# Moving the latent norms and index queries of a sparse attention ahead of the early merge products

## The chip, the cores and the metric

The kernel runs on one core of a Trainium2 chip. The metric is the device time of one execution in microseconds. The engines are PE (TensorE), DVE (VectorE), ACT (ScalarE), POOL (GpSimd) and SP (SyncE), whose queue issues most of the DMAs. They run side by side, each through its own list of instructions in order, and wait for each other on semaphores only.

## The reference

One decoder layer over 512 tokens of width 1024: adaLN conditioning, a mixer of three branches, and a mixture of experts with a shared expert. All data is float32. The mixer projects the normalised input h once and computes

- branch A, a gated linear attention (four heads), branch C, an mLSTM (four heads), each normalised per head and gated;
- branch B, a sparse attention over a latent. What matters of it here:

```
cq  = rms(h @ w_cq)  * norm_q      # 256 channels: "cn 0, 1"
ckv = rms(h @ w_ckv) * norm_kv     # 128 channels: "cn 2"
q_idx = (cq @ w_qi) / sqrt(32)     # 8 index heads of 32
I[t, s] = sum_h w[t, h] * relu(q_idx[t, h] . k_idx[s])      # causal
sel  = top 128 keys of I[t]
attention of 8 heads over ckv[sel], with q = cq @ w_uq taken through w_uk, and ALiBi
```

- the merge `(g_a * ya + g_b * yb + g_c * yc) @ w_o`, where each y is a branch times its up matrix and each g is a sigmoid of 1024 channels of h's projection.

Then come residual, norm, router (top 6 of 64 experts in groups), the experts and the final norm.

## The kernel before

**Layout.** Activations are held transposed, channels on the 128 partitions and 512 tokens along the free dimension, so that a projection of 128 channels is one PSUM bank of 128 x 512. Projections of h use float32 values split in two parts (hi and lo): `triple` (L892) makes hi x hi and hi x lo of eight k-tiles (16 matmuls, L899), then lo x hi (8 matmuls, L904). The hi part of each weight block is made by ACT (`split_hi`, L1393), the lo part by DVE (L1767) or, for the early gates, by POOL (`split_lo`, L718, in four pieces). Other products are plain float32, which PE makes in two passes per matmul.

**What orders the work.** `product_order()` (L57) is one list of all products, in PE's order: name, and the semaphore value that says that its result has been read. The product at place n uses PSUM bank n mod 8, and `begin` (L819) waits until the product eight places ahead in the list has been read. A product added to the list thus shifts which read every later product waits for. Weights come through a ring of three slots, loaded by SP in the order of a second list; a load waits for the last product that used the slot (L554 to L564). A few loads and waits are tied to names in this list (L569 to L598).

**The stages around the change**, in order:

1. The mLSTM loop over heads h = 0 to 3. PE makes bm, bt (bases of decay), four score tiles scC, the mean square of the head before (msC, L1014), one latent projection (kidx for h = 0, then cl0, cl1, cl2), then num (L1039) and den (L1043). DVE makes the masked scores (L2002, L2013, L2015), the variance (L1982), the copy of the latent projection (L1977), the finish of the head before (`finish_c`, L1985: reciprocal L1989, two multiplications L1990 and L1993, the last to oT[2], which counts oTC_ready), and the denominators (L2027 to L2031). ACT makes exponentials (L1510, L1516), the root (L1504), the square (L1529) and a copy (L1532).
2. "Early" merge products: four pairs of blocks n = 0 to 3 (`early_steps`, L37), each of a gate block eg (two projections, 48 matmuls, L899 and L904) and an up block eu (16 passes, L1059). ACT makes sigmoids (L1544) and copies (L1549), POOL multiplies and adds them (L739 for even n, L743 and L744 for odd n). Block 0 comes right behind the mLSTM loop, blocks 1 and 2 between index heads 1 and 2 of tiles 2 and 3, block 3 behind the products q and ql (L1106, L1113).
3. The latent norms: squares of the three raw latents (ACT, L1553), their sums over channels (PE, msq L1067 and mskv L1070), roots (ACT, L1556), reciprocals and multiplications to cn (DVE, L2046, L2048). The index weights w are transposed (wi, L1075) and scaled to wcol (L2039), w_uk is transposed (uk, L1080), so is cn 2 (ckr, L1085). The index queries are qi0 and qi1 (L1090), copied by ACT (L1564).
4. Index scoring and selection, for tiles i = 1, 2, 3 of 128 queries (tile 0 keeps all its keys): eight heads ix (PE L1101, relu on ACT L1575 into one of two buffers, weighted sum on DVE L2062 and L2064), then sixteen rounds of MAX8 and MATCH_REPLACE8 (L2070, L2071), a threshold (L2072) and a predicated copy of distances (L2074).
5. q and ql, early block 3, then the logits (L1123 on PE, L2096 and L2099 on DVE, exponentials L1594 on ACT), the transposes of the weights and the sums over keys.

In the code before, DVE does stage 3 behind the whole of branch C:

```
            variance_c(3)
            finish_c(3)
            dve.wait_ge(sem("oTC_ready"), 4)
            v.tensor_copy(wi0[:, :], small[32:40, :]).then_inc(sem("wi0_ready"), 1)
            b = done(dve, "wi")
```

and PE's order there is msC3, early gates 0, msq, mskv, early ups 0, wi, uk, ckr, qi0, qi1, then the index heads. SP loads w_uq, w_uk, w_uv and w_qi behind oTC_ready 4 (L578 to L584), ahead of the ring load wgE1.

## Time and profile before

| What | Value |
|---|---|
| Median of 3 runs | 1457.63 us (1456.39 to 1460.25) |
| The profiled execution | 1462.21 us, span of its instructions 1460.4 us |
| Mean granted TensorE clock | 0.948 |
| PE busy | 1334.4 us, 91% of the span |
| DVE busy | 1038.5 us, 71% |
| ACT busy | 778.6 us, 53% |
| POOL busy | 432.5 us, 30% |

The profile is one execution of the program; times in it are microseconds from the span's start. Matmuls are pipelined and their ends are modelled: a row of PE that merges several overlaps the row behind it a little. PEclk is the TensorE clock that was granted, 1.00 being 2.4 GHz and 0.50 being 1.2 GHz. In a timeline, the bracket at the end of a row is the engine's idle time before it, and what ended it. The experts, the last stage, take up the greater part of the span; the change lies between 300 and 460 us.

### The profile page before, as it was taken

The numbers are of one execution on the slowest core, as the hardware profiler recorded it, in microseconds if no ns is written. First come the engines' busy times: TensorE is split into PE (matmuls) and PEld (weight loads), VectorE is DVE, ScalarE is ACT, GpSimd is POOL, SyncE is SP. The second block draws the span as 40 slices with busy tenths as digits, with TensorE's granted clock in tenths as the row PEclk, the third lists the DMA queues.
The fourth block names the chain that finished last, engine by engine and source line by source line (L and its number), as shares of the span: only waits on it lengthen the run. The fifth ranks groups of instructions, "written<-read, shape, count | busy, mean of one in ns | idle before, by whom it ended". The sixth has DMA issues, their size and how long they took to land.

```text
span 1460.4 us, 19415 instructions
## 1 busy us (share of the span) xinstructions
PE 1334.4 (91%) x6398; PEld 1023.7 (70%) x6398; DVE 1038.5 (71%) x1302; ACT 778.6 (53%) x952; POOL 432.5 (30%) x321
## 2 busy tenths in 40 slices
PE   4897888998788979998997999999999999999986
PEld 2686678665445547887974888787788888888842
DVE  1538585375798645544467898888889999998927
ACT  3613332343233443222132888888788888888811
POOL 1100010002221000000001366665656666666610
PEclk8897989889898989999998999999999999999998
DMA  9233312103023505324134999999999999999856
GB/s 300 80 102 133 116 29 87 44 15 108 20 81 130 188 15 175 107 93 159 37 130 155 330 389 412 396 384 371 341 360 387 366 350 360 359 359 358 319 214 254
DMA packets 126617, 314.57 MB, mean 215 GB/s; under 512 B 24229, under 2 KB 61418, under 8 KB 118122
## 3 DMA queue, kind: packets, MB, share of 16 engines
q1 hardware_dynamic: 108282, 288.73, 54.6%
q0 software_dynamic: 18288, 25.21, 4.8%
q8 instruction: 30, 0.49, 0.1%
q14 instruction: 17, 0.14, 0.0%
HBM read 316.49 MB, written 38.80 MB: 243 GB/s over the span
## 4 chain that ended last, share of the span: by engine, by line
PE 62%; DMA 13%; DVE 13%; issue 5%; ACT 4%; POOL 2%; SPq 1%; POOLq 0%; DVEq 0%; ACTq 0%
PE bank L899 15%; PE bank L1285 9%; PE bank L1313 7%; PE bank L904 7%; DMA arena<-h_dram,tok_of 6%; PE bank L1289 5%; DMA ring<-in_exp_w_up 4%; PE bank L1272 3%; DVE arena L2071 2%; DVE top L2070 2%; DMA ring<-in_w_in 1%; PE bank L1354 1%; DMA arena<-in_ada_w 1%; PE bank L846 1%; PE bank L1142 1%
## 5 line engine op out<-in xcount | busy, mean ns | idle before, releaser
L2325 DVE TENSOR_TENSOR ring_parts<-ring,arena_parts 128x2048 fp32r<-128x2048 f32 x186 | 423.2, 2289 | 59.0 <-ACT arena_parts L1670 56.5
L1670 ACT ACTIVATE arena_parts<-ring 128x2048 fp32r<-128x2048 f32 x186 | 356.0, 1930 | 41.2 <-DMA ring<-in_exp_w_up 39.7
L1285 PE MATMUL bank<-arena_parts,oTA_parts 128*128 128x512 f32 x496 | 200.0, 403 | 2.7 <-DVE oTC_parts L2341 1.5
L1285 PE MATMUL bank<-arena_parts,oTC_parts 128*128 128x512 f32 x496 | 194.7, 393 | 0.0
L1313 PE MATMUL bank<-arena_parts,oTB_parts 128*128 128x512 f32 x496 | 161.3, 407 | 5.1 <-DVE ring_parts L2325 5.1
L899 PE MATMUL bank<-hT_parts,ring_parts 128*128 128x512 f32 x344 | 145.9, 424 | 7.4 <-ACT arena L1575 3.7
L794 POOL DMA_INDIRECT y_dram<-arena,row_of x62 | 96.3, 1553 | 176.9 <-ACT arena L1697 173.8
L769 POOL DMA_INDIRECT arena<-h_dram,tok_of x61 | 129.4, 2121 | 54.5 <-POOL tok_of L781 51.0
L899 PE MATMUL bank<-x_parts,ring_parts 128*128 128x512 f32 x344 | 139.1, 404 | 0.0
L1289 PE MATMUL bank<-ring_parts,oTA_parts 128*128 128x512 f32 x496 | 133.9, 392 | 0.0
L1397 ACT ACTIVATE ring_parts<-ring 128x2048 fp32r<-128x2048 f32 (+1 forms) x38 | 64.7, 1709 | 104.6 <-DMA ring<-in_w_in 57.3
L781 POOL COPY tok_of<-toks 128x1 int32 (+1 forms) x61 | 113.2, 1856 | 18.4 <-PE bank L1272 18.3
L1285 PEld LDWEIGHTS bank<-arena_parts,oTA_parts 128*128 128x128 f32 x496 | 94.2, 190 | 22.2 <-issue 3.8
L1289 PEld LDWEIGHTS bank<-ring_parts,oTA_parts 128*128 128x128 f32 x496 | 93.5, 189 | 20.7
L1285 PEld LDWEIGHTS bank<-arena_parts,oTC_parts 128*128 128x128 f32 x496 | 93.8, 189 | 17.9
L1313 PEld LDWEIGHTS bank<-arena_parts,oTB_parts 128*128 128x128 f32 x496 | 90.3, 192 | 21.9 <-issue 5.4
L1313 PE MATMUL bank<-ring_parts,oTB_parts 128*128 128x512 f32 x248 | 99.2, 400 | 0.0
L1771 DVE TENSOR_TENSOR ring_parts<-ring,ring_parts 128x2048 fp32r<-128x2048 f32 (+1 forms) x34 | 68.0, 2006 | 43.5 <-ACT ring_parts L1397 43.2
L899 PEld LDWEIGHTS bank<-hT_parts,ring_parts 128*128 128x128 f32 x344 | 68.2, 198 | 29.8 <-issue 7.9
L904 PE MATMUL bank<-hT_parts,ring_parts 128*128 128x512 f32 x344 | 85.0, 389 | 0.0
L760 POOL MEMSET row_of<- 128x1 int32 x2 | 0.2, 104 | 280.2 <-DVE x L2180 280.2
L2341 DVE TENSOR_TENSOR oTC_parts<-bank,oTA_parts 128x512 fp32r<-128x512 f32 x124 | 79.4, 681 | 5.3 <-ACT oTA_parts L1676 5.3
(421 smaller groups left out, 2299.5 us busy)
## 6 DMA issues: line engine op xcount, KB each, us to landing
ring<-in_exp_w_gate SPq DMA_DIRECT2D x124, 512.0 KB
ring<-in_exp_w_up SPq DMA_DIRECT2D x124, 512.0 KB
ring<-in_exp_w_down SPq DMA_DIRECT2D x62, 1024.0 KB
ring<-in_w_in SPq DMA_DIRECT2D x25, 1024.0 KB, 5.4
ring<-in_ada_w SPq DMA_DIRECT2D x16, 1024.0 KB, 5.8
arena<-in_ada_w SPq DMA_DIRECT2D x4, 2048.0 KB, 16.8
x<-in_x SPq DMA_DIRECT2D x2, 2048.0 KB, 12.2
ring<-in_w_o SPq DMA_DIRECT2D x4, 1024.0 KB, 5.4
```

The source lines that it names most:

```text
L769: g.indirect_dma_start(out=xg[b], out_offset=None, in_=h_dram[:, :], in_offset=bass.IndirectOffsetOnAxis(ap=rows if rows is not None else ...
L781: g.tensor_copy(dst[:, :], lists[:, bass.ds(u, 1)]).then_inc(sem("list_copied"), 1)
L794: g.indirect_dma_start(out=y_dram[:, :], out_offset=bass.IndirectOffsetOnAxis(ap=row_of[b][:, 0:1], axis=0), in_=ys[b], in_offset=None, bo ...
L899: mm(out, w if weights_left else t, t if weights_left else w, start=(j == 0 and k == 0), stop=False)
L904: ins = mm(out, w if weights_left else t, t if weights_left else w, start=False, stop=(j == n - 1))
L1285: mm(out_gu, t[c][:, tile_cols(4 * k + j)], hi[:, :, j, :], start=(k == 0 and j == 0 and x_ == 0), stop=False)
L1289: ins = mm(out_gu, xe_hi[c][:, tile_cols(4 * k + j)], lo[:, :, j, :], start=False, stop=(k == 1 and j == 3))
L1313: ins = mm(bank[4 + n][:, :], s_, w, start=(q == 0), stop=(q == 5))
L1670: A(w_hi[c][k], w_raw[c][k], ACT.Copy).then_inc(sem("gu_hi_ready" if k < 2 else "down_hi_ready"), 1)
L1771: v.tensor_tensor(lo_view(name, 1, n), ring_view(name, 0, 1, n), hi_view(name, 1, n).bitcast(F32), ALU.subtract).then_inc(sem("lo_split"), 1)
L2325: v.tensor_tensor(w_lo[c][k], w_raw[c][k], w_hi[c][k].bitcast(F32), ALU.subtract).then_inc(sem("gu_lo_ready" if k < 2 else "down_lo_ready" ...
L2341: v.tensor_tensor(xe_lo[c][:, s_], bank[half][:, :], xe_hi[c][:, s_].bitcast(F32), ALU.subtract).then_inc(sem("xe_lo_ready"), 1)
```

## The change

It moves stage 3 forward and spreads the early products otherwise.

- Each latent's square is made on ACT right behind its copy, inside the mLSTM loop (h = 1, 2, 3). msq is made by PE in the block of h = 3 ahead of cl2, its root on ACT there too; mskv comes behind msC3.
- DVE makes latent norm 0 (cn 0, 1) ahead of finish_c(3), and latent norm 1 behind it. wi0 is copied ahead of variance_c(3).
- PE's order behind the loop is early gates 0, wi, qi0, qi1, index heads. ckr moves to the start of tile 2's heads, uk to ahead of head 2 of tile 3.
- Early up blocks move: block 0 ahead of tile 2's heads, block 1 ahead of tile 3's heads, block 2 between heads 3 and 4 of tile 3. The gate blocks stay between heads 1 and 2. ACT's copies follow them; the split of wgE1 moves to tile 2's start; ukT is copied by ACT instead of DVE.
- w_qi is loaded ahead of w_cl1 on SP's queue, the other three weights where they were.
- Memory: dqC, sqB, rsB and w_qi get other places in the arena, free at those times.

The diff, cut to its core (a bracket stands for lines that are the same in both places):

```diff
--- product_order()
+        out += [("msq", "root_ready", 8)] if h == 3 else []
         out += [(f"cl{h - 1}", "craw_ready", h) if h else ("kidx", "kidx_ready", 1)]
...
+    out += [("mskv", "root_ready", 10)]
     out += early(0, "eg")
-    out += [("msq", "root_ready", 9), ("mskv", "root_ready", 10)]
-    out += early(0, "eu")
-    out += [("wi", "wcol_ready", 1), ("uk", "ukT_ready", 1)]
-    out += [("ckr", "ckr_ready", 1)]
+    out += [("wi", "wcol_ready", 1)]
     out += [(f"qi{m}", "qi_ready", m + 1) for m in range(2)]
...
-            out += early(i - 1, "eg") + early(i - 1, "eu") if i > 1 and h == 2 else []
+            out += [("ckr", "ckr_ready", 1)] if i == 2 and h == 0 else []
+            out += early(i - 2, "eu") if i > 1 and h == 0 else []
+            out += early(i - 1, "eg") if i > 1 and h == 2 else []
+            out += early(2, "eu") if i == 3 and h == 4 else []
+            out += [("uk", "ukT_ready", 1)] if i == 3 and h == 2 else []
--- memory
-        hD, dqC = rc.take(T), rc.take(T)
+        hD, dqC = rc.take(T), arena[:, 3 * T:4 * T]
...
+        sqB = arena[:, END - 3 * T:END].rearrange("p (k t) -> p k t", t=T)
+        rsB = [sqB[:, 0, :], sqB[:, 2, :]]
+        w_qi = arena[:, 20352:20864].rearrange("p (k n) -> p k n", k=2)
--- SP
+                if name == "w_cl1":
+                    sp.wait_ge(sem("oTA_ready"), 4)
+                    sp.wait_ge(sem("mb_ready"), 3)
+                    sp.dma_start(w_qi, ...)
                 if name == "wgE1":
                     sp.wait_ge(sem("oTC_ready"), 4)
+                    sp.wait_ge(sem("extra_loaded"), 48)
...
-                    sp.dma_start(w_qi, ...)
--- PE
-                pe.wait_ge(sem("squares_ready"), h + 5)
+                pe.wait_ge(sem("squares_ready"), (5, 6, 8, 10)[h])
...
                 if h:
                     mean_square(h - 1)
+                if h == 3:
+                    pe.wait_ge(sem("squares_ready"), 9)
+                    b = begin("msq")
+                    for k in range(2):
+                        ins = mm(b[:, :], ones[:, :], sqB[:, k, :], start=(k == 0), stop=(k == 1))
+                    end(ins)
...
             mean_square(3)
+            pe.wait_ge(sem("squares_ready"), 11)
+            b = begin("mskv")
+            end(mm(b[:, :], ones[:, :], sqB[:, 2, :], start=True, stop=True))
             early_gates(0)
-            (msq, mskv, early_ups(0))
             (wi)
-            (uk, ckr)
+            pe.wait_ge(sem("cn_ready"), 1)
+            pe.wait_ge(sem("extra_loaded"), 48)
             (qi0, qi1)
             for i in range(1, TT):
                 for h in range(8):
+                    if i == 2 and h == 0:
+                        (wait for cn_ready 2, ckr)
+                    if i > 1 and h == 0:
+                        early_ups(i - 2)
                     if i > 1 and h == 2:
                         early_gates(i - 1)
-                        early_ups(i - 1)
+                    if i == 3 and h == 4:
+                        early_ups(2)
+                    if i == 3 and h == 2:
+                        (uk)
--- ACT
                 if h:
                     root_c(h - 1)
-                else:
+                if h == 3:
+                    root_b(0)
...
                 A(hC, b[:, :], ACT.Copy).then_inc(sem("hC_ready"), 1)
+                if h:
+                    act.wait_ge(sem("craw_ready"), h)
+                    A(sqB[:, h - 1, :], craw[:, h - 1, :], ACT.Square).then_inc(sem("squares_ready"), 1)
                 if h == 2:
                     split_hi("wgE0")
             root_c(3)
+            root_b(1)
...
             early_sigmoids(0)
-            split_hi("wgE1")
-            early_copies(0)
-            (copy of ckr)
             (copies of qi0, qi1)
             for i in range(1, TT):
                 for h in range(8):
+                    if i == 2 and h == 0:
+                        split_hi("wgE1")
+                        (copy of ckr)
+                        act.wait_ge(sem("cn_ready"), 2)
+                    if i > 1 and h == 0:
+                        early_copies(i - 2)
                     if i > 1 and h == 2:
                         early_sigmoids(i - 1)
                         split_hi(f"wgE{i}")
-                        early_copies(i - 1)
+                    if i == 3 and h == 4:
+                        early_copies(2)
+                    if i == 3 and h == 2:
+                        (copy of uk to ukT)
--- DVE
-                dve.wait_ge(sem("root_ready"), h + 5)
+                dve.wait_ge(sem("root_ready"), (5, 6, 7, 9)[h])
...
+            v.tensor_copy(wi0[:, :], small[32:40, :]).then_inc(sem("wi0_ready"), 1)
             variance_c(3)
+            latent_norm(0)
             finish_c(3)
             dve.wait_ge(sem("oTC_ready"), 4)
-            v.tensor_copy(wi0[:, :], small[32:40, :]).then_inc(sem("wi0_ready"), 1)
+            latent_norm(1)
             (wcol)
-            (ukT copy; for n in range(2): wait for root_ready n + 9, latent norm n)
```

The new helpers: ACT's `root_b(n)` waits for msq or mskv and writes the root to rsB[n]; DVE's `latent_norm(n)` waits for root_ready (8, 10)[n], makes the reciprocal and the one or two multiplications to cn, and counts cn_ready.

## Rows read from the trace of the kernel before

**Rows 1.** The page, part 4: the chain that ended last, by engine.
```profile
PE 62%; DMA 13%; DVE 13%; issue 5%; ACT 4%; POOL 2%; SPq 1%; POOLq 0%; DVEq 0%; ACTq 0%
```

**Rows 2.** Stretches: us, then busy us (count) of PE, PEld, DVE, ACT, POOL, PEclk, DMA.
```profile
326.00:328.00 2.00, 2.00 (x6) 1.17 (x4) 0.64 (x2) 1.99 (x4) 2.00 (x2) 0.50 0.00 0
...
348.00:380.00 32.00, 20.58 (x69) 10.38 (x67) 11.92 (x11) 10.42 (x16) 11.21 (x8) 0.79 0.38 123
...
380.00:403.00 23.00, 21.05 (x88) 13.34 (x84) 21.38 (x60) 7.81 (x15) 7.80 (x7) 1.00 0.18 55
...
431.00:463.00 32.00, 27.27 (x104) 17.64 (x104) 30.52 (x60) 13.14 (x23) 5.08 (x4) 0.99 0.21 71
```

**Rows 3.** Timeline of DVE: start, us, operation, [idle before <-releaser].
```profile
331.69 0.29 DVE L2015 SCALAR_TENSOR_TENSOR arena<-bank,arena 128x128 f32<-128x128 f32 x1
...
334.40 0.69 DVE L1977 COPY oTB<-bank 128x512 f32<-128x512 f32 x1 [1.83 <-PE bank L904]
...
335.01 3.34 DVE L1989 RECIPROCAL arena<-arena 128x512 f32<-128x512 f32 x1
...
342.07 0.69 DVE L1982 SCALAR_TENSOR_TENSOR arena<-bank,arena 128x512 f32<-128x512 f32 x1
...
347.64 0.69 DVE L1993 TENSOR_TENSOR oTC<-arena 128x512 f32<-128x512 f32 x1
...
360.27 0.19 DVE L2039 TENSOR_SCALAR wcol<-bank 128x32 f32<-128x32 f32 x1 [11.42 <-PE bank L1075]
...
370.74 0.75 DVE L2048 SCALAR_TENSOR_TENSOR arena<-oTB,par,arena 128x512 f32<-128x512 f32 x1
...
380.09 0.35 DVE L2062 TENSOR_SCALAR arena<-arena,wcol 128x256 f32<-128x256 f32 x1 [8.12 <-ACT arena L1575]
...
462.71 0.29 DVE L2096 SCALAR_TENSOR_TENSOR arena<-arena,bank 128x128 f32<-128x128 f32 x1
```

**Rows 4.** Timeline of PE; a merged row's pieces overlap the next row's.
```profile
338.52 1.02 PE L1014 MATMUL bank<-arena,ones 128*128 128x512 f32 x2
...
350.28 1.88 PE L1067 MATMUL bank<-arena,ones 128*128 128x512 f32 x4
...
352.86 7.03 PE L1059 MATMUL bank<-oTA,ring 128*128 128x512 f32 x16
...
372.46 5.79 PE L1090 MATMUL bank<-arena 128*128 128x512 f32 x8
...
378.94 2.35 PE L1101 MATMUL bank<-oTB,arena 32*128 32x256 f32 x20 [0.69 <-ACT arena L1564]
...
425.96 3.70 PE L1106 MATMUL bank<-arena 128*128 128x512 f32 x8
...
436.53 3.79 PE L1113 MATMUL bank<-arena 64*128 64x512 f32 x16 [0.77 <-issue]
...
458.15 1.95 PE L1123 MATMUL bank<-arena 128*128 128x128 f32 x16
```

**Rows 5.** Timeline of ACT.
```profile
358.24 1.91 ACT L1397 ACTIVATE ring_parts<-ring 128x2048 fp32r<-128x2048 f32 x1 [2.09 <-DMA ring<-in_w_in]
...
392.44 0.60 ACT L1544 ACTIVATE arena<-bank 128x512 f32<-128x512 f32 x1 [4.84 <-PE bank L904]
```

**Rows 6.** Timeline of DVE inside the selection.
```profile
395.37 0.43 DVE L2070 MAX8 top<-arena 128x8 f32<-128x256 f32 x1
...
402.69 1.42 DVE L2062 TENSOR_SCALAR arena<-arena,wcol 128x384 f32<-128x384 f32 x1
...
430.84 0.48 DVE L2062 TENSOR_SCALAR arena<-arena,wcol 128x512 f32<-128x512 f32 x1
...
431.35 5.48 DVE L2064 SCALAR_TENSOR_TENSOR arena<-arena,wcol 128x512 f32<-128x512 f32 x7
```

**Rows 7.** Timeline of POOL beside the selection.
```profile
394.97 4.95 POOL L725 TENSOR_TENSOR ring_parts<-ring,ring_parts 128x512 fp32r<-128x512 f32 x4 [26.41 <-ACT ring_parts L1397]
...
402.63 1.26 POOL L743 TENSOR_TENSOR arena<-arena 128x512 f32<-128x512 f32 x1
```

More of the change, by code:

```diff
@@ L1062, in _ @@
             early_gates(0)
-            pe.wait_ge(sem("squares_ready"), 11)
-            b = begin("msq")
-            for k in range(2):
-                ins = mm(b[:, :], ones[:, :], sqB[:, k, :], start=(k == 0), stop=(k == 1))
-            end(ins)
-            b = begin("mskv")
-            end(mm(b[:, :], ones[:, :], sqB[:, 2, :], start=True, stop=True))
-            early_ups(0)
             pe.wait_ge(sem("wi0_ready"), 1)
@@ L1076, in _ @@
             end(ins)
-            pe.wait_ge(sem("extra_loaded"), 96)
-            b = begin("uk")
-            for m in range(4):
-                ins = nc.tensor.transpose(b[:, tile_cols(m)], w_uk[:, tile_cols(m)], ident[:, :])
-            end(ins)
-            pe.wait_ge(sem("cn_ready"), 2)
-            b = begin("ckr")
-            for i in range(TT):
-                ins = nc.tensor.transpose(b[:, tile_cols(i)], cn[:, 2, tile_cols(i)], ident[:, :])
-            end(ins)
+            pe.wait_ge(sem("cn_ready"), 1)
+            pe.wait_ge(sem("extra_loaded"), 48)
             for m in range(2):
@@ L1504, in root_c, with root_b @@
                 A(rsC, rsC, ACT.Sqrt).then_inc(sem("root_ready"), 1)
+            def root_b(n):
+                b = done(act, ("msq", "mskv")[n])
+                A(rsB[n], b[:, :], ACT.Sqrt, scale=1.0 / (256, 128)[n], bias=epsc[:, 0:1]).then_inc(sem("root_ready"), 1)
             for h in range(4):
@@ L1549, in early_copies @@
                     A(upE[:, r, :], b[:, :], ACT.Copy).then_inc(sem("eup_ready"), 1)
-            for n in range(3):
-                act.wait_ge(sem("craw_ready"), n + 1)
-                A(sqB[:, n, :], craw[:, n, :], ACT.Square).then_inc(sem("squares_ready"), 1)
-            for n, name in enumerate(("msq", "mskv")):
-                b = done(act, name)
-                A(rsB[:, n, :], b[:, :], ACT.Sqrt, scale=1.0 / (256, 128)[n], bias=epsc[:, 0:1]).then_inc(sem("root_ready"), 1)
             early_sigmoids(0)
-            split_hi("wgE1")
-            early_copies(0)
-            b = done(act, "ckr")
-            A(ckr, b[:, :].rearrange("p (i k) -> p i k", i=TT), ACT.Copy).then_inc(sem("ckr_ready"), 1)
             for m in range(2):
@@ L1569, in _ @@
                         split_hi(f"wgE{i}")
-                        early_copies(i - 1)
+                    if i == 3 and h == 4:
+                        early_copies(2)
+                    if i == 3 and h == 2:
+                        b = done(act, "uk")
+                        A(ukT, b[:, :].rearrange("p (i h) -> p i h", i=4), ACT.Copy).then_inc(sem("ukT_ready"), 1)
                     n = 8 * (i - 1) + h
```

37 lines of the change are left out of this document (24 added, 13 removed).

## The prediction

> **What bounds the kernel now.** I read the chain that ended last, then the table of stretches, then the four engines' timelines from 320 to 470 us. The chain [rows 1] is mostly PE over the whole span, but that is the expert stage; around the change another engine carries it. The stretches [rows 2] show it: DVE is busy for 21.38 of the 23 us from 380 on and for 30.52 of the 32 us up to 463. That is the selection of keys for query tiles 1, 2 and 3, one chained instruction after another, and nothing else can shorten it. Ahead of it, from 348 to 380, no engine but PE is over 40% busy and PE itself stands idle for a third: this is the gap that the change attacks. In it [rows 3] DVE has finished branch C at 348.3, waits for PE's transpose until 360.27, makes both latent norms (two reciprocals of 3.35 us) until 371.5, and starts the first index head at 380.09, after the transposes of ckr, the qi products and their copies [rows 4]. Whatever brings 380.09 forward moves everything behind it, if PE and ACT still deliver the later index heads in time. After the selection the logits follow at 462.71 [rows 3]; PE had finished the last early product at 458.15 [rows 4], 4.5 us earlier.
>
> **The change, part by part.** Times are on the axis of the profiled execution.
>
> *Block 3 of mLSTM.* The squares of the latents move into it: three ACT squares at 0.6 us, as ACT's other operations on 512 columns [rows 5]. Those after blocks 1 and 2 lie where ACT waits for DVE, except that the second pushes the exponentials of block 3 by 0.5 us, and with them the last masked score tile, from 332.0 [rows 3] to 332.5. PE takes in the msq product here: four passes, 1.88 us [rows 4]. This has a hidden price. Banks go round by eight in the order of the product list. Before, cl2 stood eight behind den2; with msq ahead of it, it stands eight behind bm3, whose bank counts as free only with SW_ready 16, the last score tile. So cl2 doesn't follow msq at once but starts at 332.5, with PE idle for about 3 us. The clock was already down near here (0.50 in 326 to 328 [rows 2]), and after an idle stretch eight passes took 5.79 us where eight like them took 3.70 at full clock [rows 4]: a toll of 2.1, bounds 0 and 2.1, of which I take all, for PE does nothing in the wait. cl2's 24 matmuls are half a gate block (11.3 us for 48, see below), 5.5 us at an even pace. It ends at 332.5 + 5.5 + 2.1 = 340.1, not just ahead of DVE's copy at 334.40 [rows 3], so at 334.2: 5.9 us later.
>
> *From there to the first index head.* DVE: copy of cl2, finish of head 2 and the denominator took 334.40 to 342.07, 7.7 us [rows 3], so 348.0. Then the copy of wi0 and the variance, 1.1; latent norm 0: 3.35 + 2 x 0.75 = 4.85, which gives cn 0 and 1 at 353.9; the finish of head 3, 4.8 (oTC_ready 4 at 358.8, not 348.3); latent norm 1, 4.1; wcol and the mask 0.8. DVE is ready at 363.7. PE: num3, den3, msC3 end at 345.4; mskv waits for the third square, which stands on ACT behind oTC_ready 3 and the copy of hC: 347.0. Behind this wait the whole early gate block is queued. mskv 0.9, gates 11.3 (from half a microsecond into the row of 338.52 to 350.28 [rows 4]), wi 0.4, the qi products at full clock 3.7: 363.3. From the end of qi1 to the first head's start and to DVE's use of it, 0.7 and 1.15 [rows 3, 4]: 365.1. PE sets it, DVE is 1.4 us early. ACT's early sigmoids wait for oTC_ready 4 at 358.8, need a table load and end at 361.2, before it must copy qi0 at 361.5: hidden, with 0.3 us to spare. **Start of scoring: 380.1 to 365.1, minus 15.0.** If cl2 restarts at full clock it is minus 17.1; if the gates also pay a toll after their short wait, minus 12.9.
>
> *DMAs.* w_qi's load goes ahead of w_cl1's, some 80 us before it is used; its ring wait is not touched. Behind oTC_ready 4, now 10.5 us later, stand on SP's queue the three weights, wgE1 and wuE1. In the profile the weights of wgE1 were there at 358.24 [rows 5], 9.9 us after oTC_ready 4; now about 369. ACT asks for them after tile 1's heads, 4 us behind the start of scoring, at 369; PE needs them at 374. Nothing, with 5 us to cover it.
>
> *Tile 1 and the start of tile 2.* Between heads 1 and 2 of two tiles PE has one gate and one up block, 18.3 us, as before, but the up block now lies ahead of heads 0 and 1. The removed part: DVE's ops around 400 to 405 were stretched by POOL's four products L743 and L744: TENSOR_SCALAR on 384 columns 1.42 us against 0.48 for 512 columns later [rows 6], while one of POOL's ran (402.63, 1.26 us [rows 7]). Four such, 0.9 to 1.0 each: **minus 3.7**. These products come now while DVE is in MAX8 and MATCH_REPLACE8; MAX8 took its 0.43 us beside POOL's split at 395.37 too [rows 6, 7]. The added part: PE reaches ix22 at 365.1 + 0.7 (ckr) + 7.0 + 11.3 + 0.6 = 384.7; ACT then does the sigmoid and the 1.91 us split of wgE2 [rows 5] before its relu, so DVE gets head 2 at 387.8. DVE has done 20.9 us of tile 1 and two heads by 386.9: **plus 0.9**, bounds 0 and 2.
>
> *POOL's split under the scoring of tile 2.* The split wgE2 on POOL, 4 pieces in 4.95 us [rows 7], starts when ACT's does end, 387.3: exactly where DVE makes the six remaining scalar_tensor_tensor with two SBUF inputs. Before, the splits lay under MAX8. The price is bounded by nothing (DVE wins) and by 4 x 1.24 = 5.0. I play it through with one operation at a time: **plus 3.7**, near the upper end, since the rows [rows 6, 7] show the first L2062 held until POOL's operation was all but over. The Trainium skill, "SBUF — State Buffer", section "Who interferes with whom", says that a VectorE instruction with two SBUF inputs and a GpSimd instruction that reads SBUF exclude each other for the whole instruction. By that rule this term is the 3.7; if they shared the port it would be under 1, and the forecast some 3 us lower. The trace agrees with the rule [rows 6, 7].
>
> *Tile 3.* The up copies of block 2 (two ACT copies, 0.6 each) and POOL's two products now fall between its heads 3 and 4. ACT's cadence there is already the limit (5.48 us for seven heads [rows 6]); POOL holds off two heads. **Plus 2.0**, bounds 0.5 and 2.5.
>
> *PE ahead of the logits.* q0 must now wait for ix32's relu and q2, q3 for the copies of block 2; PE has been idle before it, so toll 2.1 again. Counted from DVE's start of tile 3 (430.84 [rows 6]), q starts at 1.3 and takes 2 x 3.7 + 2.1, so ql starts at 11.0, where it was 436.53 - 430.84 = 5.7 [rows 4]; then ql 3.7, gates and ups 11.3 + 7.0. The last up ends at 33.0; DVE is through at 462.71 - 430.84 + 2.0 = 33.9: the former cover of 4.5 us is down to about 1. POOL's last products then touch DVE's threshold op: **plus 0.3**, bounds 0 and 3.
>
> **Sum:** -15.0 - 3.7 + 0.9 + 3.7 + 2.0 + 0.3 = -11.8 us. Everything from the logits on is the same chain, shifted; the ada loads there hang on the same products, with less lead but still ahead. The profiled execution took 1462.21 us (span 1460.4), 4.6 over the median of the runs: it should become 1450.4, and the median 1457.63 - 11.8 = **1445.8 us**.
>
> **Rivals.**
> - *Forecast*, minus 9 to minus 15: chance 0.50.
> - *No tolls.* cl2 restarts fast (-2.1), POOL's split misses the scoring (-3.7), ix22 is in time (-0.9): 1439. For it: the phase between DVE and POOL is decided within 1 us. Against: the stretched operation [rows 6]. Chance 0.20.
> - *PE becomes the bound at the logits* or pays the clock toll twice more (gates at 348, gates at tile 3): 3 to 6 us back, 1449 to 1452. For it: only 1 us of cover. Chance 0.18.
> - *The change does not do what it says*: the bank wait of cl2 and the wait of mskv hold PE, and the head start is given back to the selection, where DVE waits for ix22 and ix34. It needs 8 us more than I charge: within 0.3% (4.4 us, about what a measurement of this kernel can tell from no change), 1457. Chance 0.07.
> - *Slower.* PE runs the early blocks among the index heads at the lower clock level (1.2 GHz). The block of 18.3 us before ix22 becomes up to 36.6, against 20.9 us of DVE work: DVE would wait 18 us, more at ix32. That is over the 11.8 gained once a block spends about 12 us more; 1464. Against it: the granted clock was 1.00 in 380 to 403 with the same blocks [rows 2]; for it: 0.79 in 348 to 380. Chance 0.05.
>
> **The numbers.** Faster by over 0.3%: 0.50 + 0.20 + 0.18 = 0.88; within: 0.07; slower: 0.05. The range takes in the forecast's bounds, most of the second case and the third: 1440.0 to 1451.8.
>
> **What would show it.** Right: the first L2062-like op 13 to 17 us earlier; PE idle before cl2 at about 329.5 to 332.5; oTC_ready 4 after the first latent norm; six stretched scoring ops of tile 2 beside POOL's L725; the last early up about a microsecond before the logits. Wrong: cl2 at 328; scoring bound by DVE's norms instead of PE's gates; DVE waiting for PE over 2 us anywhere between the first head and the logits; time lost or won after the logits.

## The result, and the profile after

The changed kernel took 1443.01 us (median of 4 runs, 1436.76 to 1445.17) beside 1457.01 (4 runs, 1453.32 to 1460.25) for the kernel before: ratio 0.9876, 95% interval 0.9831 to 0.992. It is faster, by 18 us if the ratio is taken at its middle, by 12 to 25 with the interval; the two medians lie 14.0 us apart. Two more measurements of the same kernel, told below, gave 0.9908 and 0.9897; the three together put the gain at about 15 us.

The profiled execution took 1442.98 us, its span is 1441.2 us. The lines of the changed kernel are shifted: scoring is L2095 and L2097 (before L2062 and L2064), threshold and predicated copy L2105 and L2107, triple's two loops L911 and L916, the early split on POOL L737, its products for odd blocks L755 and L756. From the page, busy time and chain by engine:

```profile
PE 1320.2 (92%) x6398; PEld 1012.3 (70%) x6398; DVE 1040.7 (72%) x1301; ACT 777.9 (54%) x953; POOL 436.0 (30%) x321
...
PE 60%; DMA 14%; DVE 12%; issue 5%; ACT 5%; POOL 2%; SPq 1%; POOLq 0%; DVEq 0%; ACTq 0%
```

The chain [rows 1] has lost 2% of PE and 1% of DVE, which says little. The stretches of the stages around the change say more (us, then busy us and count of PE, PEld, DVE, ACT, POOL, PEclk, DMA):

```profile
330.00:355.00 25.00, 22.67 (x99) 14.93 (x98) 22.99 (x21) 7.14 (x12) 2.65 (x2) 1.00 0.20 64
...
355.00:376.00 21.00, 21.00 (x85) 13.38 (x84) 19.44 (x60) 8.84 (x15) 7.50 (x6) 1.00 0.33 104
...
376.00:407.00 31.00, 28.61 (x100) 15.98 (x98) 29.06 (x59) 8.86 (x15) 16.01 (x12) 1.00 0.33 105
...
407.00:443.00 36.00, 32.52 (x116) 19.12 (x120) 33.83 (x62) 14.22 (x25) 8.19 (x6) 0.95 0.21 71
```

Before, DVE did 11.92 us of work in the 32 us ahead of the scoring, and PE ran with a mean granted clock of 0.79 [rows 2]. Now DVE is busy for 22.99 of 25 us there and the clock is 1.00. (It was lower just ahead of this window, under cl2: 0.77 from 322.80 to 330.18, see below.) The hole is closed. DVE's timeline shows how, and what it cost further on:

```profile
322.45 0.29 DVE L2046 SCALAR_TENSOR_TENSOR arena<-bank,arena 128x128 f32<-128x128 f32 x1
...
330.18 0.69 DVE L2008 COPY oTB<-bank 128x512 f32<-128x512 f32 x1 [6.84 <-PE bank L916]
...
342.29 1.42 DVE L2069 SCALAR_TENSOR_TENSOR arena<-oTB,par,arena 128x512 f32<-128x512 f32 x2
...
347.79 0.69 DVE L2024 TENSOR_TENSOR oTC<-arena 128x512 f32<-128x512 f32 x1
...
352.62 0.18 DVE L2082 TENSOR_SCALAR wcol<-bank 128x32 f32<-128x32 f32 x1
...
354.70 0.35 DVE L2095 TENSOR_SCALAR arena<-arena,wcol 128x256 f32<-128x256 f32 x1 [1.30 <-ACT arena L1606]
...
375.57 0.41 DVE L2095 TENSOR_SCALAR arena<-arena,wcol 128x384 f32<-128x384 f32 x1
...
377.18 7.27 DVE L2097 SCALAR_TENSOR_TENSOR arena<-arena,wcol 128x384 f32<-128x384 f32 x6 [0.54 <-ACT arena L1606]
...
384.48 1.32 DVE L2101 COPY_PREDICATED arena<-future,negc 128x128 f32<-128x128 int32 x1
...
406.72 0.47 DVE L2095 TENSOR_SCALAR arena<-arena,wcol 128x512 f32<-128x512 f32 x1
...
410.24 4.24 DVE L2097 SCALAR_TENSOR_TENSOR arena<-arena,wcol 128x512 f32<-128x512 f32 x4 [0.69 <-ACT arena L1606]
...
439.12 1.50 DVE L2105 TENSOR_SCALAR oTB<-arena 128x512 int32<-128x512 f32 x1
...
440.66 1.67 DVE L2107 COPY_PREDICATED arena<-oTB,arena 128x512 f32<-128x512 int32 x1
...
442.36 0.29 DVE L2129 SCALAR_TENSOR_TENSOR arena<-arena,bank 128x128 f32<-128x128 f32 x1
```

cl2 is copied at 330.18 and the first scoring operation comes at 354.70, 24.52 us later; before it was 45.69 (334.40 to 380.09 [rows 3]). Both multiplications of latent norm 0 stand at 342.29, ahead of the finish of head 3 (347.79). PE's side of it:

```profile
317.40 1.88 PE L1044 MATMUL bank<-arena,ones 128*128 128x512 f32 x4
...
322.80 0.50 PE L911 MATMUL bank<-hT_parts,ring_parts 128*128 128x512 f32 x1 [3.52 <-DVE arena L2046]
...
336.85 1.13 PE L1066 MATMUL bank<-arena,ones 128*128 128x512 f32 x2 [1.53 <-ACT arena L1561]
...
349.17 3.70 PE L1095 MATMUL bank<-arena 128*128 128x512 f32 x8
...
407.94 8.83 PE L1126 MATMUL bank<-arena 128*128 128x512 f32 x16 [3.32 <-ACT arena L1606]
...
438.21 1.95 PE L1143 MATMUL bank<-arena 128*128 128x128 f32 x16
```

msq at 317.40 is followed by 3.52 us of waiting, until DVE's last masked score tile (322.45, L2046) frees the bank for cl2 at 322.80. And POOL beside the selection:

```profile
376.84 5.89 POOL L737 TENSOR_TENSOR ring_parts<-ring,ring_parts 128x512 fp32r<-128x512 f32 x4 [9.21 <-ACT ring_parts L1417]
...
384.35 1.29 POOL L755 TENSOR_TENSOR arena<-arena 128x512 f32<-128x512 f32 x1 [1.62 <-issue]
...
439.08 1.26 POOL L755 TENSOR_TENSOR arena<-arena 128x512 f32<-128x512 f32 x1 [0.82 <-ACT arena L1579]
...
440.42 1.32 POOL L756 TENSOR_TENSOR arena<-arena 128x512 f32<-128x512 f32 x1
```

The split at 376.84 lies over DVE's six scoring operations at 377.18, which took 7.27 us; the product at 384.35 over the predicated copy at 384.48; the last two over the threshold operations at 439.12 and 440.66.

**Where the time came from.** The table cuts the span at starts of DVE's operations: the mLSTM loop's first (its base, L2002 before), the denominator of head 2, the first scoring operation of tiles 1, 2 and 3, the first logit, the split of the attention's output into its lo part (L2132 before), and the list of tokens with which the experts' part begins (L2298 before). The kernel before has two profiled executions, the changed one three.

| Stretch, us | before | before again | after | again | third | change of the means |
|---|---|---|---|---|---|---|
| span's start to loop | 276.1 | 273.9 | 269.5 | 275.0 | 270.6 | -3.3 |
| loop to denominator of head 2 | 47.1 | 43.9 | 43.9 | 47.1 | 45.5 | 0.0 |
| to the first scoring operation | 56.9 | 57.1 | 41.2 | 39.6 | 39.6 | -16.9 |
| tile 1 | 22.6 | 22.6 | 20.9 | 20.9 | 20.9 | -1.7 |
| tile 2 | 28.2 | 28.1 | 31.2 | 31.2 | 31.2 | +3.0 |
| tile 3, to the first logit | 31.9 | 31.9 | 35.6 | 34.4 | 35.7 | +3.3 |
| to the attention's output | 84.4 | 82.3 | 82.7 | 84.0 | 82.4 | -0.3 |
| to the list of tokens | 235.8 | 234.1 | 236.5 | 237.2 | 236.3 | +1.7 |
| to the span's end | 677.5 | 678.5 | 679.6 | 679.0 | 678.6 | +1.1 |
| span | 1460.4 | 1452.4 | 1441.2 | 1448.3 | 1440.7 | -13.0 |

The four stretches that the change touches give -12.2 us (139.6 to 127.4), -10.6 to -13.7 in every pair of executions. The first pair of spans differs by 19.2 us, but 6.6 of these are gone before the mLSTM loop begins and 3.1 more ahead of the denominator of head 2. Up to the loop the two programs differ by one DMA only, the load of w_qi (issued at 243.26 in the changed kernel). That load did not make the difference: the weight load that SP issues at 165.42 and 162.20 in the two profiles before comes at 156.76, 164.23 and 159.97 after, and from it to the loop all five take 110.6 to 112.8 us. Behind the first logit 1.1 us are lost in the first pair, 2.5 us in the means.

### The profile page after: what moved, and what is told of

Same layout as the page of the kernel before. It is cut to its first block, busy times and chain, and to the rows that moved or that the text cites. A ratio compares the mean times of both kernels' runs of the same rounds, so it can differ in the third digit from the quotient of the medians.

```text
span 1441.2 us, 19418 instructions
## 1 busy us (share of the span) xinstructions
PE 1320.2 (92%) x6398; PEld 1012.3 (70%) x6398; DVE 1040.7 (72%) x1301; ACT 777.9 (54%) x953; POOL 436.0 (30%) x321
## 4 chain that ended last, share of the span: by engine, by line
PE 60%; DMA 14%; DVE 12%; issue 5%; ACT 5%; POOL 2%; SPq 1%; POOLq 0%; DVEq 0%; ACTq 0%
PE bank L911 15%; PE bank L1305 10%; PE bank L916 7%; PE bank L1333 7%; DMA arena<-h_dram,tok_of 5%; PE bank L1309 5%; DMA ring<-in_exp_w_up 5%; PE bank L1292 3%; PE bank L1230 2%; DVE arena L2104 2%; DMA arena<-in_ada_w 1%; PE bank L1374 1%; DVE top L2103 1%; DMA ring<-in_w_in 1%; PE bank L858 1%
## 5 line engine op out<-in xcount | busy, mean ns | idle before, releaser
L806 POOL DMA_INDIRECT y_dram<-arena,row_of x62 | 99.2, 1600 | 176.9 <-ACT arena L1728 174.6
L911 PE MATMUL bank<-hT_parts,ring_parts 128*128 128x512 f32 x344 | 142.7, 415 | 6.4 <-DVE arena L2046 3.5
L911 PE MATMUL bank<-x_parts,ring_parts 128*128 128x512 f32 x344 | 136.7, 397 | 0.0
L1305 PEld LDWEIGHTS bank<-arena_parts,oTA_parts 128*128 128x128 f32 x496 | 94.2, 190 | 22.6 <-issue 4.2
L911 PEld LDWEIGHTS bank<-hT_parts,ring_parts 128*128 128x128 f32 x344 | 66.5, 193 | 28.3 <-issue 6.1
L916 PE MATMUL bank<-hT_parts,ring_parts 128*128 128x512 f32 x344 | 85.0, 390 | 0.0
```

The lines of the kernel that those rows point to most:

```text
L806: g.indirect_dma_start(out=y_dram[:, :], out_offset=bass.IndirectOffsetOnAxis(ap=row_of[b][:, 0:1], axis=0), in_=ys[b], in_offset=None, bo ...
L911: mm(out, w if weights_left else t, t if weights_left else w, start=(j == 0 and k == 0), stop=False)
L916: ins = mm(out, w if weights_left else t, t if weights_left else w, start=False, stop=(j == n - 1))
L1305: mm(out_gu, t[c][:, tile_cols(4 * k + j)], hi[:, :, j, :], start=(k == 0 and j == 0 and x_ == 0), stop=False)
```

## The experiments

The theory: the stages between the mLSTM and the logits carry the whole gain, with the five terms of the sum; two of the costs (cl2's wait behind msq, POOL's split under the scoring of tile 2) are not needed. The rival: a good part of the gain comes from elsewhere, or one half of the change, the norms or the up blocks alone, carries it. Each experiment below was timed in five rounds beside the kernel before. Its profile is read by the same stretches, since one execution's span scatters more than the terms are large.

### The two kernels again

> The kernel before, unchanged, against itself. Both theories: ratio 1.000, scatter of a few microseconds. What differs: by the theory that the change is worth 10 to 12 us and the other 7 us between the two profiles are the granted clock before the mLSTM loop, DVE's first operation of the loop (L2002, 276.12 us in the profile of before, 269.53 in that of the changed kernel) moves by several microseconds between executions of this same kernel. By the rival, that the change itself makes the stages before the loop faster (w_qi's load), it stays within 1 us of 276.

> The changed kernel, unchanged. Forecast by parts (from DVE's denominator of head 2 to the first logit 10.6 us less in the profiles): 10 to 13 us faster than before, ratio 0.991 to 0.993. Rival, that the first measurement of 0.9876 holds: 17 to 19 us, ratio 0.987 to 0.988.

> The changed kernel a third time. By the sum over the stages (12.2 us as the mean of two profiles of each kernel, from head 2's denominator to the first logit) 10 to 14 us faster than before, ratio 0.990 to 0.993. By the rival, that the first ratio of 0.9876 is right and something outside these stages adds 5 us: 0.986 to 0.989.

The kernel before against itself: 0.9988 (0.9962 to 1.0014), medians 1456.83 and 1457.85, single runs from 1450.8 to 1467.5. Its loop began 2.2 us earlier than in the first profile, so it does move without the change. The changed kernel: 0.9908 (0.9876 to 0.994), median 1447.27; the third time 0.9897 (0.9854 to 0.994), median 1444.34. Both ratios lie a little below what the stages alone let one expect (0.991 to 0.993 and 0.990 to 0.993), and above what the first ratio did (0.987 to 0.988 and 0.986 to 0.989). The stretches are in the table above. The start of the scoring is 17.3 and 17.4 us nearer to the denominator of head 2 in these two, against 15.7 in the first profile. PE's row of cl2, again with msq ahead of it, in the second profile:

```profile
331.41 0.50 PE L911 MATMUL bank<-hT_parts,ring_parts 128*128 128x512 f32 x1 [1.88 <-DVE arena L2046]
```

Here the wait is 1.88 us and not 3.52, since PE had reached msq later, and no time is lost behind it. In the third profile the wait is 3.52 us as in the first, and still no time is lost:

```profile
325.45 0.50 PE L911 MATMUL bank<-hT_parts,ring_parts 128*128 128x512 f32 x1 [3.52 <-DVE arena L2046]
```

The stretch from cl2's first matmul to DVE's copy of it, in the first profile and in the third (last three numbers: PEclk, DMA share, GB/s):

```profile
322.80:330.18 7.38, 7.38 (x25) 5.95 (x26) 0.54 (x1) 1.40 (x3) 0.00 (x0) 0.77 0.00 1
```

```profile
325.45:331.23 5.78, 5.78 (x25) 4.80 (x26) 0.55 (x2) 1.39 (x3) 0.00 (x0) 1.00 0.00 1
```

So the wait for the bank is real in all three, and the clock toll of a restart is 1.6 us in one (granted clock 0.77) and none in the two others (1.00). Six of the twelve profiles below and above have msq ahead of cl2; the toll shows in two of them: 16.7 us from the denominator of head 2 to cl2's copy, against 15.1 in the other four.

### msq behind cl2

```diff
+        out += [(f"cl{h - 1}", ...)]
         out += [("msq", "root_ready", 8)] if h == 3 else []
-        out += [(f"cl{h - 1}", ...)]
...
                 if h == 0: ...
                 else: project(f"cl{h - 1}", ...)
+                if h == 3: (msq, as in the changed kernel)
                 b = begin(f"num{h}")
```

> The changed kernel with msq behind cl2 instead of ahead of it, so that cl2's bank is that of den2 again and no longer waits for the last score tile. My theory: cl2 follows msC2 at once, 5.4 us earlier, its idle time of 3.52 us and the clock toll behind it are gone, DVE copies cl2 right behind the variance; scoring starts 5 to 6.5 us earlier and the kernel is 5 to 6.5 us faster than the changed one. Rival, that the wait is covered because the finish of the heads on DVE sets the start: within 1 us of the changed kernel.

Measured: 0.9876 (0.9839 to 0.9913), median 1441.03. PE's rows of cl2's first matmul and of msq:

```profile
319.20 1.42 PE L911 MATMUL bank<-hT_parts,ring_parts 128*128 128x512 f32 x1
...
326.36 1.88 PE L1052 MATMUL bank<-arena,ones 128*128 128x512 f32 x4
```

cl2 starts right behind msC2 and msq right behind cl2, with no wait in either place. Denominator of head 2 to first scoring operation: 35.75 us against 41.23, 39.63 and 39.59 with msq in front. From cl2's copy on nothing changes (24.50). So msq's place costs 3.8 to 5.5 us here (2.2 to 3.8 by the two kernels below); the order of two products in the list, 1.88 us of work, decides it. The 5 to 6.5 us expected had been worked out from the first profile, which paid the toll; the other two did not. The runs' medians lie 6.2 us apart (1441.03 beside 1447.27, taken side by side), but the intervals of the two ratios overlap (0.9876 and 0.9908), so that the time alone doesn't part the two kernels.

### POOL's split out of the scoring

```diff
+                    if i == 3 and h == 0:
+                        split_hi("wgE2")
                     if i > 1 and h == 0:
                         early_copies(i - 2)
                     if i > 1 and h == 2:
                         early_sigmoids(i - 1)
-                        split_hi(f"wgE{i}")
+                    if i == 3 and h == 2:
+                        split_hi("wgE3")
```

> The changed kernel with ACT's split of wgE2, and so POOL's, behind the index heads of tile 2 instead of in their midst. My theory (POOL's pieces and DVE's two-input operations exclude each other): the six operations of L2097 take 3.9 instead of 7.27 us, the copy behind them 0.3 instead of 1.32, the wait of 0.54 goes; tile 2 takes 26 to 27 us instead of 31.15; 4 to 5 us faster than the changed kernel. Rival, that ACT's relus set their pace: L2097 stays at over 1 us each, tile 2 within 1 us of 31.

Measured: 0.9842 (0.9809 to 0.9876), median 1438.24. Tile 2 took 27.41 us against 31.15: 3.74 us. DVE's rows of tile 2, then POOL's split:

```profile
381.80 4.54 DVE L2100 SCALAR_TENSOR_TENSOR arena<-arena,wcol 128x384 f32<-128x384 f32 x7
...
386.37 0.31 DVE L2104 COPY_PREDICATED arena<-future,negc 128x128 f32<-128x128 int32 x1
```

```profile
387.55 5.01 POOL L737 TENSOR_TENSOR ring_parts<-ring,ring_parts 128x512 fp32r<-128x512 f32 x4 [14.15 <-ACT ring_parts L1417]
```

Seven scoring operations in 4.54 us, 0.65 each, against 1.21 each beside the split in the changed kernel (7.27 for six), and the predicated copy 0.31 instead of 1.32. The split itself now lies under the sixteen rounds of MAX8 and MATCH_REPLACE8 and takes 5.01 us, against 5.89 with its pieces among the scoring. This is the term "POOL's split" by itself, 3.7 us in the forecast. The median is 9.0 us under that of the changed kernel taken beside it, more than tile 2 explains; where the rest comes from was not found.

### Both, and block 2's copies behind the last head

The first of these two kernels has both edits above. The second also has this:

```diff
-                    if i == 3 and h == 4:
-                        early_copies(2)
...
+            early_copies(2)
             for m in range(4):
                 b = done(act, f"q{m}")
```

> The changed kernel with both edits: msq behind cl2, and the split of wgE2 behind tile 2's heads. If they add: from head 2's denominator to the first logit 119 to 120 us (123.2 and 122.6 with one of them, 126.0 and 128.9 with none), 8 us under the changed kernel, some 20 us under the kernel before: ratio 0.985 to 0.987. Rival, that PE becomes the bound ahead of the logits (the last early up has to be made by then): 122 or more, DVE idle ahead of the first logit.

> As the kernel with both edits, and ACT's copies of up block 2, and so POOL's two products, behind the last index head of tile 3 instead of between heads 3 and 4. My theory: DVE's wait of 0.7 us and the POOL pieces under its operations go, tile 3 takes 1.5 to 2.5 us less; q2 and q3 come later on PE, which has about 4 us of lead at the logits, so that nothing comes back: 1.5 to 2 us under the kernel with both edits from head 2's denominator to the first logit. Rival: the later q2 and q3 put PE's last up behind DVE's last selection, and the gain is eaten there.

Measured: 0.9831 (0.979 to 0.9872), median 1435.39, and 0.9795 (0.9758 to 0.9832), median 1431.32 (1426.13 to 1434.76). The stretch from the denominator to the first logit is 120.46 and 119.38 us. That is 6.9 and 8.0 us less than the changed kernel's mean of 127.4; 119 to 120 had been expected of the first. The two edits don't quite add: from the denominator of head 2 to cl2's copy these two kernels need 12.95 and 12.87 us, where the one with msq's edit alone needed 11.25; PE's score tile ahead of cl2 took 4.31 us for eight passes in the first of them, 2.42 in the one with msq's edit alone. The granted clock from 316 to 323 was 0.61 and 0.54 in the two, 0.76 in that one. The copies bring 1.0 us and not 1.5 to 2.5. DVE's rows of tile 3 in the second kernel:

```profile
401.73 5.48 DVE L2099 SCALAR_TENSOR_TENSOR arena<-arena,wcol 128x512 f32<-128x512 f32 x7
...
407.24 1.25 DVE L2103 COPY_PREDICATED arena<-future,negc 128x128 f32<-128x128 int32 x1
```

The scoring is even (5.48 us for seven heads, the pace before [rows 6]), but POOL's two products of block 2 have only slid on, and the predicated copy behind the scoring takes 1.25 us. This kernel is the fastest of all: its interval lies wholly below those of the second and third measurements of the changed kernel (from 0.9876 and 0.9854 up, against 0.9832 at most).

### The up blocks alone

The kernel before, with this:

```diff
-    out += early(0, "eu")
...
-            out += early(i - 1, "eg") + early(i - 1, "eu") if i > 1 and h == 2 else []
+            out += early(i - 2, "eu") if i > 1 and h == 0 else []
+            out += early(i - 1, "eg") if i > 1 and h == 2 else []
+            out += early(2, "eu") if i == 3 and h == 4 else []
```

and the same moves of `early_ups` on PE and `early_copies` on ACT; norms, ckr and uk stay where they were.

> The kernel before with only the up blocks moved: block 0 ahead of tile 2's heads, block 1 ahead of tile 3's, block 2 between heads 3 and 4 of tile 3; the norms stay where they were. If the parts add: wi comes 7 us earlier, so the norms and the first index head too (from head 2's denominator 50 us instead of 57); tile 1 20.9 to 21.3; tile 2 31.2 and tile 3 34.4 to 35.6, as in the changed kernel; from head 2's denominator to the first logit 136.5 to 137.5 instead of 139.6: 2 to 3 us faster than before. Rival, that the norms' place is all that matters at the start: scoring starts as before, and the kernel is 2 to 4 us slower than before.

Measured: 0.997 (0.9944 to 0.9997), median 1454.16. DVE's rows:

```profile
345.17 0.19 DVE L2044 TENSOR_SCALAR wcol<-bank 128x32 f32<-128x32 f32 x1 [4.55 <-PE bank L1075]
...
366.26 0.35 DVE L2067 TENSOR_SCALAR arena<-arena,wcol 128x256 f32<-128x256 f32 x1 [7.52 <-ACT arena L1580]
```

The start of the scoring is 5.6 us nearer to the denominator of head 2 (51.36 against 57.0), tile 1 is 1.7 shorter, tiles 2 and 3 give 2.7 and 3.8 back, and 0.9 us of the stretch's 139.6 are left, 1 to 2 less than expected. DVE's wait for wi fell from 11.42 to 4.55 us, and 7.52 us of waiting for ACT's relu stand ahead of the first head: the two norms, made between, now set the start (PE stands 10.74 us for them ahead of ckr, at 358.32).

### The norms alone

The changed kernel with the up blocks and their copies back (block 0 behind early gates 0, the others at h == 2):

```diff
             early_gates(0)
+            early_ups(0)
...
                     if i > 1 and h == 2:
                         early_gates(i - 1)
+                        early_ups(i - 1)
--- ACT
             early_sigmoids(0)
+            act.wait_ge(sem("cn_ready"), 2)
+            early_copies(0)
--- memory (w_qi where wi0 was, which is free there)
-        w_qi = arena[:, 20352:20864]...
+        w_qi = wi0_all[:, :]...
+        wi0 = arena[0:8, 14352:14864]
```

> The changed kernel with the up blocks back at their old places (block 0 behind its gates, ahead of wi and the index queries, blocks 1 and 2 with their gates); w_qi and wi0 have other places in memory. If the parts add: scoring starts 7 us later than in the changed kernel (46.7 to 48.3 us behind head 2's denominator), tiles 1, 2 and 3 take 22.6, 28.2 and 31.9 us as before; from that denominator to the first logit 129 to 131; 9 us faster than before. Rival, that the start of scoring is bound by the norms on DVE rather than by PE's early products: it starts within 2 us of the changed kernel, and the kernel is 14 us or more faster than before.

Measured: 0.9951 (0.9923 to 0.9979), median 1452.80; the stretch is 134.98 us, 4 more than expected at the most. PE's and DVE's rows at the start of tile 2's heads:

```profile
366.10 0.76 PE L910 MATMUL bank<-hT_parts,ring_parts 128*128 128x512 f32 x1 [3.63 <-ACT ring_parts L1414]
```

```profile
387.94 7.11 DVE L2093 SCALAR_TENSOR_TENSOR arena<-arena,wcol 128x384 f32<-128x384 f32 x6 [5.33 <-ACT arena L1602]
```

The gate block 1, without the up block in front of it, comes before its weights are split: PE stands 3.63 us for ACT's split of wgE1, and DVE 5.33 us for the relus behind it. Tile 2 took 34.76 us instead of the 28.2 expected; the start of the scoring came about as expected (46.47 us behind the denominator of head 2). So the up block of block 0 is more than work in another place: in the changed kernel it covers the arrival and the split of wgE1.

### The norms alone, with the split of wgE1 early

```diff
             act.wait_ge(sem("cn_ready"), 2)
+            split_hi("wgE1")
             early_copies(0)
...
                     if i == 2 and h == 0:
-                        split_hi("wgE1")
```

> The kernel norms_only with ACT's split of wgE1 moved ahead of the copies of up block 0 again, where the kernel before has it. In norms_only PE stood 3.63 us for that split ahead of the gates of block 1, and DVE then 5.33 us for the relus of tile 2; tile 2 took 34.76 us instead of 28.2. My theory: with the split early, tile 2 takes 28 to 29 us again, scoring starts up to 2 us later (ACT's split now lies ahead of the copies of the index queries), tile 1 22.6; from head 2's denominator to the first logit 130 to 132 us instead of 134.98, 3 to 5 us under norms_only. Rival, that PE's block between heads 1 and 2 is too long for tile 1 wherever the split lies: tile 2 stays at 33 or more.

Measured: 0.9936 (0.9907 to 0.9966), median 1450.31; the stretch is 134.23 us. ACT's row, then DVE's:

```profile
361.94 1.91 ACT L1414 ACTIVATE ring_parts<-ring 128x2048 fp32r<-128x2048 f32 x1 [8.23 <-DMA ring<-in_w_in]
```

```profile
366.99 0.86 DVE L2091 TENSOR_SCALAR arena<-arena,wcol 128x256 f32<-128x256 f32 x1 [5.98 <-ACT arena L1602]
...
367.89 6.34 DVE L2093 SCALAR_TENSOR_TENSOR arena<-arena,wcol 128x256 f32<-128x256 f32 x7
```

Tile 2 is back at 27.26 us, as expected, but the wait has only gone elsewhere. ACT stands 8.23 us for the landing of wgE1, whose load hangs on oTC_ready 4, ahead of the copies of qi0 and qi1. The scoring starts 3.0 us later (49.44 us behind the denominator of head 2, against 46.47), but only 1.3 us of this lie behind cl2's copy, where the edit acts; the other 1.6 are the slow restart of cl2, which this profile has and the one before it doesn't. The split on POOL then lies under tile 1's scoring: seven operations on 256 columns take 6.34 us, and tile 1 25.67 us instead of 20.86. Neither place is good without the up block: the weights of gate block 1 hang on oTC_ready 4, which now stands behind the first latent norm, and something has to cover that.

## Why the prediction came out as it did

In the changed stages its sign, mechanism and sum were right; its range was too narrow at the low end. The ratio of the first measurement gives 0.9876 x 1457.63 = 1439.6 us, 0.4 below the low end of 1440.0. The later two give 1444.2 and 1442.6, inside, and so is the first measurement's own median, 1443.01. That one ratio falls out by 0.4 us is less than any measurement here can tell; that the range had no room below is a fault of the forecast.

**The step that failed** is the last: the sum of the changed stages is taken from the median as it stands, and "The range takes in the forecast's bounds, most of the second case and the third." Everything outside these stages is a term put at nothing, with no room around it ("Everything from the logits on is the same chain, shifted"). It measured otherwise. In the first pair of profiles the stages give 10.6 us, less than the 11.8 forecast, and all of the excess lies outside them: 6.6 us ahead of the mLSTM loop, 3.1 in the loop up to the denominator of head 2, and 1.1 lost behind the logits. In the means it is 3.3, 0.0 and 2.5 lost. The stretch ahead of the loop took 267.1 to 276.1 us in twelve profiled executions (271.0 to 276.1 in the three without w_qi's early load, 267.1 to 275.0 in the nine with it). The sum was also set against one median of three runs. With 3 us more for it, less than half of what the loop's start alone moves by, the low end would have been 1437.

**The terms:**

- *Start of the scoring, -15.0.* Measured -15.7, -17.3 and -17.4, in the means -16.9: the term of the sum that was furthest off. The bank wait of cl2 was there as worked out, on the last masked score tile. Its toll had been taken whole, 2.1; it was 1.6 once and nothing twice. So the case "if cl2 restarts at full clock it is minus 17.1" is the usual one. PE's gates and the qi products, not DVE's norms, set the start, and DVE's idle time there was 1.30 us against 1.4 worked out. The rest is as forecast too: wcol at 352.62 is done 1.9 us ahead of the first head.
- *Tiles 1 and 2, -3.7 and +0.9 and +3.7, together +0.9.* Measured -1.7 and +3.0, together +1.3. Taken apart by the experiments: POOL's split costs 3.74 us (31.15 to 27.41), so what is left, 20.85 + 27.41 - 50.75 = -2.5, is the contention removed and ix22 late, -2.8 in the forecast. DVE's wait for ix22 was 0.54 us. The Trainium skill, "SBUF — State Buffer", section "Who interferes with whom", had this right for the operation with two SBUF inputs: 1.21 us each beside POOL, 0.65 without it. The rows shown before the forecast ([rows 6], L2062) are of a TENSOR_SCALAR with one tensor input, so they did not yet show this for two; the experiment does. Among the costs that it added, the forecast charged the scoring only; the predicated copies suffer as well.
- *Tile 3, +2.0.* The scoring from its first operation to its end took 7.8 us against 6.0, +1.8.
- *Ahead of the logits, +0.3.* Measured +2.0, +0.7 and +2.0, inside the bounds of 0 and 3, but most of it not for the reason worked out. PE was not late: it starts the logits' first products at 438.21, 4.1 us before DVE wants them at 442.36, not 1 us, for q took 8.83 us where 9.5 had been taken, and the last up block ended 1.5 us sooner. The cost lay in POOL. Its last two products fell exactly on the threshold operation (1.50 us against 0.44 undisturbed) and on the predicated copy (1.67 against 0.73). In the second profile POOL's pair began 1.8 us ahead of the threshold operation, and only that one was held: 1.13 us, and 0.73 for the copy.
- *Sum.* -11.8 forecast, -12.2 measured in these stages. The start brought up to 2.4 us more than forecast, the time ahead of the logits cost up to 1.7 more, so a part of the agreement is luck.
- *Behind the logits, nothing.* "Time lost or won after the logits" was named as a sign of being wrong, and it came: 2.5 us are lost in the means, of which the stretch up to the list of tokens has 1.7. The last section says where.
- *Loads.* In the forecast the weights of wgE1 are there 9.9 us behind oTC_ready 4, and nothing waits for them. In the changed kernel ACT's split of them begins 9.6 us behind it (358.08), without idle time ahead of it: right, and close. The two experiments without the up block show what the cover is worth: 3.6 us of PE and 5.3 of DVE. Of the ada loads, called "still ahead", one was late by 0.66 us on PE, at 452.35.

**The rivals.** "No tolls" was half right: cl2 did restart fast in two profiles of three, while POOL's split did not miss the scoring. PE didn't become the bound at the logits. DVE waited at most 0.69 us between the first head and the first logit, so the head start was not given back. The blocks among the index heads ran at a granted clock of 1.00 (355 to 407) and 0.95 (407 to 443), which rules out the slow case. That one half of the change carries the gain is not what the stretches show: alone, the up blocks bring 0.9 us of the stretch and the norms 4.6 (5.4 with the early split, about 7 without that profile's slow restart of cl2), together 12.2. This rests on one profile of each half; the ratios of the norms alone (0.9951 and 0.9936) are above those of the whole, but their intervals overlap with its later two.

**What stays open.** The mean of three ratios, 0.9894, is 15.5 us, the profiles' mean 13.0, the stages alone 12.2. Each interval holds all three. Whether the 3.3 us ahead of the loop are chance or an effect of the program's layout on that stretch was not settled. They are there before w_qi's load, the one operation in which the two kernels differ ahead of the loop.

## What to carry to other kernels

When a consumer's inputs are moved forward, ask of each block that stood there whose arrival it covered: here the moved up block covered the landing and split of the next weights, and the two halves alone brought 0.9 and some 5 to 7 of the 12.2 us. Read a rotation of buffers by its list: one small product put in front of a larger one made the larger wait for a later reader, 2 to 5 us that a change of places gave back. Place the second engine's elementwise work by what the first does at that moment, scoring or sorting, and expect two executions of the same program to differ by more than such a step is worth, so give the range room for that.

## What the runs showed of the hardware

**The predicated copy is held by POOL too.** Beside a product or split piece of POOL it took 1.32 us for 128 columns against 0.31 without, 1.46 against 0.45 for 256 (401.33 in the kernel before, 375.23 in the changed one), 1.67 against 0.73 for 512. With the split late, MAX8 on 384 columns took 0.56 us and MATCH_REPLACE8 0.54, beside POOL's split (387.97) and behind it (397.98) alike; a reciprocal took 3.35 us beside a split before (361.58) as without one (3.34 [rows 3]).

**A spell of low clock that came with the phase.** From the merge's output to the list of tokens the kernel before took 85.4 and 85.9 us, and the changed one 89.3, 89.1 and 88.8, with the same instructions. The stretch from 50 to 60 us into it, in the changed kernel:

```profile
722.00:732.00 10.00, 10.00 (x42) 8.97 (x42) 1.41 (x16) 4.54 (x8) 0.00 (x0) 0.50 0.32 116
```

The same stretch in the kernel before, and in the one with both edits and the copies late:

```profile
748.00:758.00 10.00, 10.00 (x50) 6.97 (x49) 4.99 (x52) 4.30 (x8) 0.00 (x0) 0.95 0.25 97
```

```profile
714.00:724.00 10.00, 10.00 (x49) 7.28 (x48) 4.37 (x49) 4.54 (x8) 0.00 (x0) 0.90 0.35 129
```

PE is busy for all 10 us in each, but at a granted clock of 0.50, that is 1.2 GHz, in the changed kernel (42 matmuls), and at 0.95 and 0.90 in the others (50 and 49). The last-named kernel took 85.4 us for the stage. So about 3.4 us of what the changed kernel had won were lost 280 us further on, in all three of its profiles.

All twelve profiles together say more. Six take 88.8 to 89.4 us for this stage and have the granted clock of 0.50 from 50 to 60 us into it, six take 84.9 to 85.9 us and have 0.87 to 1.00 there. The longer six are those in which the stage begins (at the first L2178 in the kernel before, the same operation in the others) between 670.3 and 680.2 us; the shorter six begin at 664.2 and 666.7, or at 682.9 to 697.6. Kernels with the norms moved are on both sides. So in these runs the time at which the stage begins parts the two groups, and the edit does not. No run tests it by shifting the stage on purpose, and what in the chip decides it stays open.

**The same wait may cost the clock or not.** cl2 after 3.52 us of idle PE took 7.38 us to its copy in one execution of the changed kernel (granted clock 0.77) and 5.78 us in another (1.00). In both, PE had been busy without a gap for the 7.4 us ahead of msq, at 1.00. After 1.88 us of idle PE it took 5.78 us too.
